# Gated linear attention heads scored by levels: factors carried from level to level, both directions in one product

## What is computed

```python
def gla_scan(k, v, log_a, s0, q=None):
    '''S_t = diag(a_t) S_{t-1} + k_t v_t^T ; o_t = S_t^T q_t'''
    ...
        bcum = jnp.cumsum(ac, axis=2)
        b_end = bcum[:, :, -1, :]
        k_to_end = kc * jnp.exp(b_end[:, :, None, :] - bcum)
        s_new = jnp.exp(b_end)[..., None] * s + jnp.einsum('bhik,bhiv->bhkv', k_to_end, vc)
        rel = jnp.where(tril[:, :, None], bcum[:, :, :, None, :] - bcum[:, :, None, :, :], -jnp.inf)
        scores = jnp.einsum('bhjk,bhik,bhjik->bhji', qc, kc, jnp.exp(rel))
        o = (jnp.einsum('bhji,bhiv->bhjv', scores, vc)
             + jnp.einsum('bhjk,bhkv->bhjv', qc * jnp.exp(bcum), s))
```

## Time and profile before

| | us |
|---|---|
| runs of the kernel before: median (lowest, highest) | 2446.46 (2445.9, 2447.78) |
| the profiled execution, its own time | 2447.49 |
| its span in the trace | 2445.7 |
| PE busy in the span | 2386.6 (98%) |
| DVE busy in the span | 1686.0 (69%) |
| ACT busy in the span | 1134.6 (46%) |
| DMA queue 1, share of the 16 engines | 64.4% |

### The profile page before, as it was taken

The page is one execution under the profiler, slowest core; times in us unless marked ns, Lnnn a source line. Parts: engine busy times, 40 slices in busy tenths (PEclk is TensorE's granted clock), DMA queues, the critical chain, the costliest instruction groups (busy, mean ns, idle before and its releaser), DMA issues.

```text
span 2445.7 us, 31233 instructions
## 1 busy us (share of the span) xinstructions
PE 2386.6 (98%) x12012; PEld 2018.7 (83%) x12012; DVE 1686.0 (69%) x2069; ACT 1134.6 (46%) x1403; POOL 0.2 (0%) x4
## 2 busy tenths in 40 slices
PE   8998999999999999999999999899999999999997
PEld 6887888888888888887788887777888888888886
DVE  5435688877877877647467745674788658875785
ACT  5434545445445346544354444363444434443443
POOL 0000000000000000000000000000000000000000
PEclk9999999999999999999999999999999999999999
DMA  8662677877878877549459866045566666666664
GB/s 294 194 193 74 228 258 282 302 281 284 290 276 293 294 277 281 171 144 370 163 181 355 314 191 201 14 122 188 155 189 189 193 210 188 188 193 190 190 186 132
DMA packets 136036, 532.97 MB, mean 218 GB/s; under 512 B 19041, under 2 KB 19169, under 8 KB 122737
## 3 DMA queue, kind: packets, MB, share of 16 engines
q1 hardware_dynamic: 135920, 531.38, 64.4%
HBM read 529.21 MB, written 2.11 MB: 217 GB/s over the span
## 4 chain that ended last, share of the span: by engine, by line
PE 93%; DVE 3%; ACT 1%; issue 1%; DMA 1%; SPq 0%; ACTq 0%; DVEq 0%
PE PSA L705 22%; PE PSA L608 18%; PE PSA L610 18%; PE PSA L609 18%; PE PSA L701 6%; PE PSA L708 6%; DMA raw<-in_w_in 1%; PE PSA L743 1%; PE PSA L926 1%; DVE XX L1964 0%; DVE u L1822 0%; PE PSA L1016 0%; PE PSA L653 0%; PE PSA L888 0%; PE PSA L770 0%
## 5 line engine op out<-in xcount | busy, mean ns | idle before, releaser
L1698 DVE TENSOR_TENSOR wlo<-raw,whi 128x1024 fp32r<-128x1024 f32 x788 | 933.0, 1217 | 397.5 <-ACT whi L1165 396.3
L1165 ACT ACTIVATE whi<-raw 128x1024 fp32r<-128x1024 f32 x788 | 800.3, 1052 | 496.9 <-DMA raw<-in_w_down 182.6
L705 PE MATMUL PSA<-u,whi 128*128 128x512 f32 x2400 | 573.8, 391 | 0.0
L705 PEld LDWEIGHTS PSA<-u,whi 128*128 128x128 f32 x2400 | 440.8, 188 | 85.3 <-DVE u L1822 0.2
L608 PE MATMUL PSA<-whi,u 128*128 128x512 f32 x1088 | 428.2, 394 | 7.6 <-DVE wlo L1698 5.1
L610 PE MATMUL PSA<-whi,u 128*128 128x512 f32 x1088 | 426.1, 392 | 0.0
L609 PE MATMUL PSA<-wlo,u 128*128 128x512 f32 x1088 | 425.8, 391 | 0.0
L608 PE MATMUL PSA<-whi,ahi 128*128 128x512 f32 x856 | 333.4, 389 | 0.0
L609 PE MATMUL PSA<-wlo,ahi 128*128 128x512 f32 x856 | 333.0, 389 | 0.0
L610 PE MATMUL PSA<-whi,alo 128*128 128x512 f32 x856 | 333.0, 389 | 0.0
L608 PEld LDWEIGHTS PSA<-whi,u 128*128 128x128 f32 x1088 | 205.8, 189 | 54.7 <-issue 6.0
(11 more groups left out here) (299 smaller groups left out, 1368.8 us busy)
## 6 DMA issues: line engine op xcount, KB each, us to landing
raw<-in_w_up SPq DMA_DIRECT2D x300, 512.0 KB, 3.7
raw<-in_w_in SPq DMA_DIRECT2D x208, 512.0 KB, 4.3
raw<-in_w_down SPq DMA_DIRECT2D x192, 512.0 KB, 4.2
mod_slot<-in_w_mod_rows SPq DMA_DIRECT2D x90, 1024.0 KB, 6.1
raw<-in_w_out SPq DMA_DIRECT2D x64, 512.0 KB, 3.6
raw<-in_w_down2b SPq DMA_DIRECT2D x20, 512.0 KB, 3.6
raw<-in_w_mod SPq DMA_DIRECT2D x12, 512.0 KB, 4.3
h<-in_x SPq DMA_DIRECT2D x2, 1024.0 KB, 6.2
```

Of the source, the lines that this page charges most:

```text
L705: mm = pe.matmul(both, wh[:, c], u_pair[:, k, :], start=k == 0, stop=k == KD - 1)
L1165: AF(whi[:, n % SLOTS, 0:w], raw[:, n % SLOTS, 0:w], ACT.Copy).then_inc(hi_done, 1)
L1698: TT(wlo[:, n % SLOTS, 0:w], raw[:, n % SLOTS, 0:w], whi[:, n % SLOTS, 0:w], ALU.subtract).then_inc(lo_done, 1)
```

## The change

Instead of exponentials at each level, ACT makes the per-token factors `EA` once (PE now only transposes `log_a`: `token_decay`). Keys and queries of both directions lie in `KZ` and `QZ` and are multiplied from level to level by the factor of the sibling block; `GL[L]` holds the products of the factors of each block of L tokens, one doubling per level (`doubled`). At a level half of the tokens of each direction are active, so one product serves both directions: the keys of both are put together in `KA` by ACT (`mixed_keys`), the queries are picked by an access pattern (`active`), and `take` copies all 1024 elements of a tile row under one mask. The work is done in two halves of two heads. For levels 5 and 6 ACT copies the blocks without a mask (`take_far`). What `QZ` holds behind the last level is what `qB` held. The mask table is half as long.

```diff
@@ tiles @@
-        lev_in = z_at("lev_in", [P, 2 * LEVELS * P], F32, 60 * K)
+        lev_in = z_at("lev_in", [P, LEVELS * P], F32, 60 * K)
+        EA = z_at("EA", [P, 2, H, TOK], F32, 0, True)
+        QZ = z_at("QZ", [P, 2, H, TOK], F32, 8 * K, True)
+        KZ = z_at("KZ", [P, 2, H, TOK], F32, 16 * K, True)
+        KA = z_at("KA", [P, H, TOK], F32, 74 * K)
+        ONE = H * TOK
+        def active(x, lev, hd, t):
+            L = 2 ** lev
+            dims = [[2 * L, P // (2 * L)], [ONE + L, 2], [1, L]]
+            return strided(x[:, :, :, :], hd * TOK + t * P, [d for d in dims if d[1] > 1])
+        def active_half(x, lev, half):
+            L = 2 ** lev
+            n = ONE // 2
+            return strided(x[:, :, :, :], half * n, [[ONE + L, 2], [2 * L, n // (2 * L)], [1, L]])
+        def siblings(lev, half, first):
+            L = 2 ** lev
+            n = ONE // (2 * L)
+            g = GL[L]
+            begin, step = (1, 2 * n - 1) if first == 0 else (2 * n + 1, -2 * n - 1)
+            return strided(g, half * n + begin, [[step, 2], [2, n // 2], [0, L]])
@@ PE @@
+            token_decay(0, 6)
+            token_decay(1, 4)
             pe.wait_ge(acc_free, BY["out2"].blk0)
             transposed(0, 0, B["gqt_ready"])
             transposed(6, 2, B["gqt_ready"])
-            running_decay(1, 4)
+            pe.wait_ge(B["gqt_dve"], 1)
             pe.wait_ge(B["gqt_act"], 1)
+            own_scores()
+            for lev in range(LEVELS):
+                for half in range(2):
+                    pe.wait_ge(B["qe_done"], 2 * lev + half + 1)
+                    if lev == 0:
+                        pe.wait_ge(B["cum_done"], 2)
+                    else:
+                        pe.wait_ge(B["ka_done"], 2 * lev + half - 1)
+                    if lev >= 2:
+                        pe.wait_ge(B["lv_done"], lev - 1)
+                    level_scores(lev, half)
+                if lev == 0:
                     key_decay(0)
                     key_decay(1)
                     pe.wait_ge(B["dg_done"], 1)
                     gate_matrix_rows(1, 0)
...
+                if 1 <= lev <= GLA_UNITS:
+                    if lev >= 2:
+                        mod_columns(5, heads.unit0 + lev - 2, apart=True)
+                    fill_tiles(heads, lev - 1, 4)
+                if lev == 1:
                     transposed(1, 0, B["mt_ready"])
+                if lev == 2:
                     transposed(7, 0, B["mt_ready"])
+                if lev == 4:
+                    mod_columns(5, heads.unit0 + 2, apart=True)
...
+                if lev == 5:
                     pe.wait_ge(B["gc_done"], 1)
                     first_state(0)
+                if lev == 6:
                     pe.wait_ge(B["s1_done"], 1)
                     first_state(1)
...
+            pe.wait_ge(B["lv_done"], NEAR)
+            pe.wait_ge(B["far_done"], LEVELS - NEAR)
+            pe.wait_ge(B["qe_done"], 2 * LEVELS + 2)
@@ ACT @@
+                for z in range(2):
+                    act.wait_ge(B["cum_ready"], z + 1)
+                    AF(EA[:, z, :, :], PSA[:, 6 - 2 * z:8 - 2 * z, :], ACT.Exp, scale=1.0 / 16.0).then_inc(B["cum_done"], 1)
+                act.wait_ge(B["gqt_ready"], 2)
+                for z in range(2):
+                    AF(KZ[:, z, :, :], PSA[:, 2:4, :], ACT.Copy).then_inc(B["gqt_act"], 1)
+                def mixed_keys(lev):
+                    for half in range(2):
+                        act.wait_ge(B["k_upd"], 2 * lev + half - 1)
+                        if lev >= 2:
+                            act.wait_ge(B["lv_ready"], 2 * lev + half - 1)
+                        AF(KA[...], active_half(KZ, lev, half), ACT.Copy).then_inc(B["ka_done"], 1)
+                mixed_keys(1)
+                [kte, kte1: Exp] mixed_keys(2); gla_rows(0); [mqT]; mixed_keys(3); [rows2: Exp]; gla_rows(1); [mkT]
+                mixed_keys(4); gla_rows(2); masks(); row_highs(); mixed_keys(5); mixed_keys(6); take_far(5); take_far(6)
@@ DVE @@
+                def next_keys(lev, half):
+                    TT(active_half(KZ, lev, half), active_half(KZ, lev, half), siblings(lev, half, 0), ALU.mult).then_inc(B["k_upd"], 1)
+                def next_queries(lev, half):
+                    dve.wait_ge(B["lv_ready"], 2 * lev + half + 1)
+                    TT(active_half(QZ, lev, half), active_half(QZ, lev, half), siblings(lev, half, 1), ALU.mult).then_inc(B["qe_done"], 1)
+                def doubled(n):
+                    pairs = GL[n // 2].rearrange("p z (b e) -> p z b e", e=2)
+                    ch.link(TT(GL[n], pairs[:, :, :, 0], pairs[:, :, :, 1], ALU.mult))
+                after = {0: lambda: (add_biases(...), row_chain(0)),
+                         1: lambda: (row_chain(1), row_chain(2), keys_to_end(0), keys_to_end(1)),
+                         2: lambda: mod_adds(5, heads.unit0),
+                         3: lambda: (row_chain(3), mod_adds(5, heads.unit0 + 1)),
+                         4: lambda: (chunk_ends(), row_chain(4), mod_adds(5, heads.unit0 + 2), row_lows()),
+                         5: lambda: first_state(0),
+                         6: lambda: first_state(1)}
+                TS(gqT[:, :, :], PSA[:, 0:2, :], DK ** -0.5, None, ALU.mult).then_inc(B["gqt_dve"], 1)
+                dve.wait_ge(B["cum_done"], 2)
+                first_queries(0)
+                first_queries(1)
                 dve.wait_ge(B["dg_ready"], 1)
                 STT(STf, PSA[:, 0:2, :].rearrange("p b (c j) -> p (b c) j", j=P), 2.0, diag, ALU.mult, ALU.mult).then_inc(B["dg_done"], 1)
+                doubled(2)
+                for lev in range(LEVELS):
+                    for half in range(2):
+                        if lev < LEVELS - 1:
+                            next_keys(lev, half)
+                    for half in range(2):
+                        next_queries(lev, half)
+                    if lev < NEAR:
+                        take(lev)
+                        doubled(4 * 2 ** lev)
+                    after[lev]()
```

More of the change, by code:

```diff
@@ L33 @@
 LEVELS = 7
+NEAR = 5
 NEG = -1.0e30
@@ L435, in program, with strided @@
                 at_ += p.iters * p.blocks
[L437 to L449, removed]
+        def strided(x, offset, dims):
+            return bass.AP(x.tensor, x.offset + offset, [list(x.ap[0])] + [list(d) for d in dims])
+        def active(x, lev, hd, t):
[12 more added lines that the diff above has]
+            return strided(g, half * n + begin, [[step, 2], [2, n // 2], [0, L]])
         def tp_banks(j):
@@ L945, in _ @@
             transposed(6, 2, B["gqt_ready"])
-            running_decay(1, 4)
+            pe.wait_ge(B["gqt_dve"], 1)
             pe.wait_ge(B["gqt_act"], 1)
[L948 to L956, removed]
-                if m == 0:
-                    pe.wait_ge(B["cum_done"], 2)
+            own_scores()
@@ new lines, in take_far @@
+                def take_far(lev):
+                    L = 2 ** lev
+                    b0 = 2 if lev % 2 else 6
+                    act.wait_ge(B["dg_done"], 1)
+                    act.wait_ge(B["lv_ready"], 2 * lev + 2)
+                    src = PSA[:, b0:b0 + 2, :].rearrange("p b (c j) -> p (b c) j", j=P)
+                    dst = ST[:, :, :, :].rearrange("p e t j -> p (e t) j")
+                    for p0 in range(0, P, L):
+                        other = p0 + L if p0 // L % 2 == 0 else p0 - L
+                        ins = AF(dst[p0:p0 + L, :, other:other + L], src[p0:p0 + L, :, other:other + L], ACT.Copy)
+                    ins.then_inc(B["far_done"], 1)
@@ new lines, in heads2 @@
+                mixed_keys(1)
+                for z in range(2):
+                    act.wait_ge(B["kt_ready"], z + 1)
+                    AF((kte1 if z else kte)[:, :], PSA[:, 4 + z, :], ACT.Exp).then_inc(B["kt_exp"], 1)
+                mixed_keys(2)
+                gla_rows(0)
+                act.wait_ge(B["mt_ready"], 1)
+                AF(mqT[:, :, :], PSA[:, 0:2, :], ACT.Copy).then_inc(B["mt_act"], 1)
+                mixed_keys(3)
+                act.wait_ge(B["w_arg"], 2)
+                AF(rows2[:, 7, :], rows2[:, 8, :], ACT.Exp, scale=-1.0)
@@ new lines, in heads2 @@
+                AF(rows2[:, 10, :], rows2[:, 9, :], ACT.Exp, bias=mctx[:, 0:1]).then_inc(B["mr_exp"], 1)
+                gla_rows(1)
+                act.wait_ge(B["mt_ready"], 2)
+                AF(mkT[:, :, :], PSA[:, 0:2, :], ACT.Copy, scale=DK ** -0.5).then_inc(B["mt_act"], 1)
+                mixed_keys(4)
+                gla_rows(2)
+                masks()
+                row_highs()
+                mixed_keys(5)
+                mixed_keys(6)
+                for lev in range(NEAR, LEVELS):
+                    take_far(lev)
@@ L1988, in keys_to_end, with chunk_ends @@
+                def chunk_ends():
+                    ends = GL[P // 2].rearrange("p z (e t b) -> p z e t b", t=TC, b=2)
+                    for z in range(2):
```

(2 more changed lines are left out.)

193 lines of the change are left out of this document (55 added, 138 removed).

## The result

The change took the kernel from 2446.38 us (median of 4 runs, 2445.9 to 2447.78) to 2427.31 us (4 runs, 2425.86 to 2429.89): a ratio of 0.9921, 95% interval 0.9909 to 0.9933. Forecast were 2425.1 and "faster".

What follows compares the result with a forecast made beforehand. DVE's nearly full list between `inL` and `weights_of_head(0)` was taken as the bound. Walked against PE and ACT, the stretch ends 21.4 us earlier: 2447.49 becomes 2426.1, for the median 2425.1. Forecast 2422 to 2428, range 2421 to 2432.5.

Steps and rivals of the forecast that it cites:

- The bound: Between `inL` and `weights_of_head(0)`, DVE's list sets the time: DVE busy 59.7 of 67.2 us, close to full.
- The walk: DVE's instructions of lead-in and levels, priced and checked against PE and ACT: `weights_of_head(0)` at 1543.8 rather than 1565.2.
- rival (1): Levels 0 and 1: short runs are slow on DVE, adding 7.2 us, 2432.3; chance 0.14.
- Rival (2): Part of the stretch: TensorE's clock falls, adding 2 to 5 us, 2427 to 2430; chance 0.14.
- the cover of 1.4: Level 5: first state ready at 1536.9, DVE wants it at 1538.3; the first place to be late.
- Rival (3): All levels: halves don't overlap, each handoff PE, DVE and ACT, PE is paid in full, +11 us, 2436; chance 0.05.
- PE walk: In the levels, PE waits for queries 0.9, 1.9 and 1.7 us before levels 2, 3 and 5, never long.
- Rival (4): Slower: the clock stays at 0.50 from level 0 to the heads behind, 2454 us; chance 0.03.
- nothing behind changes: Behind `weights_of_head(0)`: the rest keeps its time, so the stretch's 21.4 us come off the whole program.
- PE's busy time flatters it: Stretch before the change: PE's 55.8 us busy include some 10 us at a granted clock of 0.50.
- the ledger of DVE alone: In the stretch, 48.1 us of work leave DVE and 28.3 come to it, about 20 us back.
- The rule on cachelines: Level 0 queries, single values 4 KB apart: products 1.9 to 3.8 us; by the rule slower, sum 2425.7.

Runs made afterwards that it cites:

- 1: The changed kernel with two more 512-element multiplications on DVE behind each of levels 0 to 4, into an unread buffer: 2434.14 us, ratio to the kernel before 0.9948.
- 3: The changed kernel with PE's products of levels 1 and 2 alone made twice: 2430.44 us, ratio to the kernel before 0.9928.
- 11: The changed kernel with all seven takes on DVE, so levels 5 and 6 are no longer copied by ACT: 2430.46 us, ratio to the kernel before 0.9937.
- 12: The changed kernel with the twelve `mixed_keys` copies moved from ACT to DVE: 2433.38 us, ratio to the kernel before 0.9948.
- 10: The changed kernel with PE reading plain contiguous queries at levels 0 and 1, backward queries there left out: 2427.69 us, ratio to the kernel before 0.9921.
- 2: The changed kernel with PE's products of levels 1 to 6 each made twice: 2433.98 us, ratio to the kernel before 0.9945.
- 4: The kernel before, with `from_mid` cut to 4 elements in 12 of 14 passes and all products kept: 2438.06 us, ratio to the kernel before 0.9963.
- 6: Over 5, PE and DVE make both first states at level 5, before the last queries: 2425.88 us, ratio to the kernel before 0.9916.
- 7: The changed kernel with the six doublings and `keys_to_end` moved from DVE to POOL: 2427.08 us, ratio to the kernel before 0.9919.
- 5: The changed kernel with ACT's masks ahead of `mixed_keys(2)` and row highs ahead of `mixed_keys(4)`: 2427.9 us, ratio to the kernel before 0.9922.
- 8: The changed kernel with the edits of 6 and 7 together: 2423.93 us, ratio to the kernel before 0.991.
- 9: Over 8, `keys_to_end` back on DVE and each POOL doubling waiting for the queries ahead of it: 2424.73 us, ratio to the kernel before 0.9908.

## Why the prediction was right

**The bound.** DVE's list, as said. Ten instructions more came out in full (1), 3.8 us of PE work at levels 1 and 2 made no wait on DVE up to level 4 (3), and the two moves of work from ACT back to DVE cost what they take on DVE, less a wait or more by the clock (11, 12).

**The walk.** On the time axis of the kernel before, DVE was predicted to enter level 0 at 1508.3 and to end the levels at 1514.5, 1521.7, 1525.7, 1529.7 and 1535.9. Measured, less the 0.61 of the later start: 1508.2, then 1514.4, 1521.7, 1525.6, 1529.8 and 1536.0. The last queries began at 1540.1 (1539.9), `weights_of_head(0)` at 1544.0 (1543.8). The stretch: 45.8 predicted, 45.96 measured.

**Terms that were off, and small.** These change nothing in the mechanism. A `take` is 1.19 by start distance and not 1.15 (five of them: 0.2). `take_far` took ACT 2.7 us rather than 2.2 and was over at 1541.6 rather than 1541 (less the 0.61), hidden all the same. Short runs cost DVE nothing else, so rival (1) fell: keys and queries of level 0 are 1.29 a pair like those of level 6. Rival (2), the dip, did come, once, for one level: 1.46 us more at level 5, against the cover of 1.4 named there. DVE could take the first state at 1538.95 and took it at 1539.13, 0.18 later. That is the forecast with the cover used up, not the rival's +2 to +5; that the dip (1.46) and the cover (1.4) were the same size was luck, as 3 and 10 show, where a dip of the same size (1.46, 1.50) on a level 5 that began 1.2 to 1.3 later cost 1.1. Rival (3): no handoff is paid twice. PE waits 1.71 and 1.88 before levels 3 and 5, where 1.9 and 1.7 were said. But the second is for ACT's `KA`, not for queries as the prediction's PE walk has it; its ACT walk had `KA` at 1533.1, and PE started there at 1533.1, less the 0.61. The wait of 0.9 before level 2 did not come, since PE was busy until then. Rival (4) had no place: the clock came back within 4 us.

**The step that did not hold to the tenth** is "nothing behind changes". The spans differ by 20.0, not 21.4. Of the rest, 0.61 is the start of the stretch, which lies between 1495.6 and 1500.51 in the table, in an order that follows no edit: scatter. 0.62 is behind the first product of `out2`. Windows of two us from that product on, first before, then after:

```profile
1610.48:1612.48 2.00, 2.00 (x7) 1.64 (x8) 1.93 (x7) 2.00 (x5) 0.00 (x0) 0.81 0.03 8
1612.48:1614.48 2.00, 2.00 (x6) 1.32 (x4) 2.00 (x6) 0.51 (x4) 0.00 (x0) 0.50 0.92 336
1614.48:1616.48 2.00, 2.00 (x8) 1.64 (x8) 1.97 (x5) 1.16 (x2) 0.00 (x0) 0.84 1.06 192
```

```profile
1589.86:1591.86 2.00, 2.00 (x5) 1.62 (x6) 1.93 (x7) 2.00 (x5) 0.00 (x0) 0.50 0.04 8
1591.86:1593.86 2.00, 2.00 (x7) 1.52 (x6) 2.00 (x6) 0.50 (x4) 0.00 (x0) 0.50 0.92 258
1593.86:1595.86 2.00, 2.00 (x7) 1.62 (x6) 1.96 (x5) 1.15 (x2) 0.00 (x0) 0.61 1.05 269
```

The clock is at 0.50 for longer after the change, behind the same idle time of PE (2.36 in both). The first 24 products of `out2` take 8.17 us rather than 7.19 by it, 0.98 more, and what follows gives 0.36 back. But the rest lies between 834.49 and 836.14 in the table, in no order of the edits either, so this too may be no more than what executions differ by. In the table the same sentence fails by more: none of the twelve experiments changed PE's list in the heads behind, and nine profiles show them 1.6 to 3.6 longer, by the half clock. The prediction had no term for a half clock behind the stretch, where PE has no slack; that the change's profile was spared it was luck. Of the 2.2 us between 2425.1 and 2427.31 the last 0.9 are these: the forecast took off the 1.0 by which the profiled execution of before lay above its median, and that of after lay only 0.1 above.

**Before the change** DVE and PE were close together (59.7 and 55.8 busy of 67.2), which the prediction read as "PE's busy time flatters it". Experiments 2 and 4 sharpen this: with the old number of products the new list gives 50.82 and not 45.96, and DVE relieved of 12.5 us in the old kernel gives 8.3. So both halves of the change were needed, and the ledger of DVE alone (20 us) agreed with the result only because PE's work fell nearly as much (17.3 us).

**The rule on cachelines** from the Trainium skill ("SBUF — State Buffer") was weighed against a level of 1.9 us. Measured are 2.82 at level 0 and 2.19 at level 1, where pairs of values stand together, against 1.95 and 2.05 with plain queries. By that rule level 0 is slower, and the trace agrees; that level 1 is slower too, by 0.14, the prediction had not drawn from it. In the sum it has no effect: DVE's take of level 0 starts 2.3 us behind the products (1508.90, 1511.22), and the gate rows behind them are through at 1512.46, 0.9 before DVE asks for them at 1513.34.

## What to carry to other kernels

Write the list of the engine that has no waits, with start distances as prices, and walk it against the others' due times; here it came within 0.2 us of 46. Before a change takes work from one of two nearly full engines, ask where the other binds: 12.5 us less on DVE alone gave 8.3. And a place that is covered by only 1 to 2 us is lost when the half clock falls on it and the engine ahead is late as well (3, 10): order the end of a stretch so that the last wait has other work beneath it, as experiment 6 did for 2.3 us.

## What the runs showed of the hardware

**Single values 4 KB apart slow a product.** A matmul record of 128x128 fp32 takes 337 ns with them and 275 without; eight products 2.82 and 1.95 us. The pattern was swapped as a whole; the distance and the step of two were not varied apart.

**DVE can stand while POOL works.** Two fp32 multiplications of 1024 on DVE took 4.09 beside 1.89 of POOL and 2.36 alone; beside an instruction that reads PSUM (1.23, 1.31) there was no loss. The Trainium skill ("GPSIMD Engine Reference", "Specifications", the row on SBUF interfaces) says that the two share them and names DVE instructions with two SBUF inputs. By that rule, the trace agrees; the size, 1.73 for 1.89, is from these runs.

**The half clock lay in another place in nearly every profile.** It lay in the lead-in and at the last levels (1), at level 5 (the change, 3 and 7), at level 3 (5), at both (10, 11), at levels 3 and 6 (12), behind the longest waits for `XX` (before the change and 4), and behind `weights_of_head(0)` in nine of the twelve; with the stretch at 1.00 throughout (2, 6, 8, 9) it came behind it in 2, 6 and 9, and only 8 had none up to `out2`. The heads behind take 45.28, about 46.95 or 48.4 to 48.9 by it, steps and not a spread. Behind which wait it comes was not settled: in 5 a wait of 1.71 stood before it, in 6 one of 1.72 stood before products of 2.05. Nor was it settled how much of this is the edit and how much the single execution, since no kernel has two profiles here. The runs say that executions differ: of nine of the kernel before, made along with 5 to 8, the five with a mean granted clock of 0.994 have spans of 2441.8 to 2443.9, and the four with 0.989 to 0.991 have 2445.8 to 2447.1. So a single profile of such a kernel can have 1.6 to 3.6 us of this in it, as much as most experiments here are about.
